# A triangular solve whose products go to PSUM, and expert outputs added to the residual rows by an accumulating scatter

## The reference, cut to what matters

```python
# chunk_gated_delta: 4 heads, both directions
lmat = jnp.where(strict, jnp.einsum('bhnid,bhnjd->bhnij', kb, k) * decay, 0.0)
tinv = lax.linalg.triangular_solve(lmat + eye, eye, left_side=True, lower=True, unit_diagonal=True)
...
# hier_moe: top-1 of 4 groups, top-2 of its 8 experts, blocks of 128 rows for one expert
hdn = jax.nn.silu(xb @ w1[e]) * (xb @ w3[e]);  y = hdn @ w2[e]
y_assign = ybuf[dest] * sw[:, None]                    # the gate
y = jax.ops.segment_sum(y_assign, stok, num_segments=n_tok)
...
x = x + hier_moe(rmsnorm(x, norm2_g), ...);  out = rmsnorm(x, final_norm_g)
```

## Time and profile before

| | |
|---|---|
| median of 3 runs | 3221.87 us (3218.67 to 3228.97) |
| the profiled execution | 3223.99 us, of which its span is 3222.4 us |
| busy in the span | PE 85%, DVE 63%, POOL 35%, ACT 31% |
| bytes moved by DMA | 433.96 MB, 135 GB/s over the span |
| `delta` | about 943 to 1680 us |
| `route` | 1975.7 to 2030 us |
| `experts` | 2030 to 3110.6 us |
| `combine` | 3110.6 to 3222.4 us |

### The profile page before, as it was taken

One profiled execution on the slowest core, in us unless ns is written; L12 is line 12 of the kernel. 1 busy time (PEld: TensorE's weight loads), 2 busy tenths in 40 slices (PEclk: granted clock), 3 DMA queues, 4 the chain that ended last, 5 costly groups with the idle time before them and its releaser, 6 DMA issues. The chain is left out here.

```text
span 3222.4 us, 45930 instructions
## 1 busy us (share of the span) xinstructions
PE 2732.1 (85%) x15152; PEld 2417.5 (75%) x15153; DVE 2039.0 (63%) x2191; ACT 1011.8 (31%) x2067; POOL 1128.5 (35%) x841
## 2 busy tenths in 40 slices
PE   5999999999858888888888995698899999999840
PEld 4998989989747777777776884576787888778730
DVE  5465564655537777777763335879678576877827
ACT  5152351523523333333323221122222323222223
POOL 4110110101035555555522221444354354435424
PEclk9999999999979999999998997799999999999975
DMA  4011120111121111111005441688567565757639
GB/s 151 27 59 41 48 67 29 58 39 48 42 83 53 53 52 52 52 52 52 27 13 173 138 154 52 240 304 317 205 251 272 208 236 215 286 208 293 235 142 359
DMA packets 228387, 433.96 MB, mean 135 GB/s; under 512 B 15065, under 2 KB 104393, under 8 KB 228170
## 3 DMA queue, kind: packets, MB, share of 16 engines
q1 hardware_dynamic: 207336, 349.86, 31.2%
q0 software_dynamic: 13328, 55.06, 4.7%
q10 hardware_dynamic: 7634, 27.79, 2.1%
HBM read 352.75 MB, written 87.25 MB: 137 GB/s over the span
## 5 line engine op out<-in xcount | busy, mean ns | idle before, releaser
L468 PE MATMUL project_proj<-hT_high,project_w_high 128*128 128x412 f32 (+3 forms) x1392 | 496.3, 357 | 28.0 <-issue 10.4
L468 PE MATMUL project_proj<-hT_low,project_w_high 128*128 128x412 f32 (+3 forms) x1392 | 474.9, 341 | 0.0
L468 PE MATMUL project_proj<-hT_high,project_w_low 128*128 128x412 f32 (+3 forms) x1392 | 474.8, 341 | 0.0
L1682 DVE TENSOR_TENSOR experts_w_low<-experts_w_whole,experts_w_high 128x2048 fp32r<-128x2048 f32 x128 | 355.6, 2778 | 4.4
L1776 PE MATMUL experts_h<-experts_w_high,experts_xT_high 128*128 x848 | 340.5, 401 | 18.8 <-DVE experts_w_low L1682 11.8
L1776 PE MATMUL experts_h<-experts_w_low,experts_xT_high 128*128 x848 | 338.9, 400 | 0.0
L1776 PE MATMUL experts_h<-experts_w_high,experts_xT_low 128*128 x848 | 337.5, 398 | 0.0
L1680 DVE CAST experts_w_high<-experts_w_whole 128x2048 fp32r<-128x2048 f32 x128 | 191.6, 1497 | 168.4 <-DMA experts_w_whole<-in_w_dram 168.3
L468 PEld LDWEIGHTS project_proj<-hT_high,project_w_high 128*128 128x128 f32 (+1 forms) x1392 | 261.4, 188 | 45.1 <-issue 31.6
L958 PE MATMUL delta_prep<-delta_Tm,delta_M 128*128 128x128 f32 x1152 | 185.1, 319 | 119.5 <-DVE delta_Tm L1117 116.9
L468 PEld LDWEIGHTS project_proj<-hT_low,project_w_high 128*128 128x128 f32 (+1 forms) x1392 | 261.3, 188 | 14.4 <-issue 9.8
(11 more groups left out here) (282 smaller groups left out, 5814.3 us busy)
## 6 DMA issues: line engine op xcount, KB each, us to landing
experts_w_whole<-in_w_dram SPq DMA_DIRECT2D x128, 1024.0 KB, 10.1
experts_w_whole<-in_w_dram SPq DMA_DIRECT2D x32, 2048.0 KB, 18.6
delta_qkv<-feat SPq DMA_DIRECT2D x36, 768.0 KB, 4.9
y_rows<-experts_yout ACTq DMA_DIRECT2D x53, 512.0 KB
project_w_whole<-in_w_tiles_dram SPq DMA_DIRECT2D x28, 512.0 KB, 4.3
feat<-project_out SPq DMA_DIRECT2D x48, 205.0 KB, 1.9
normalise_x<-in_x_dram SPq DMA_DIRECT2D x18, 512.0 KB, 3.2
delta_row<-gc_rows SPq DMA_DIRECT2D x36, 256.0 KB, 3.3
```

What stands on the lines that cost most here:

```text
L468: r = pe.matmul(dst, w[s][:, kt, 0:m], x[:, kt, lo:hi], start=kt == 0 and i == 0, stop=kt == KD - 1 and i == 2)
L1682: m = dve.tensor_tensor(low, loaded, high.bitcast(F32), ALU.subtract)
```

## The change

The 8x8 substitution writes its products to a PSUM tile of lane 1 that is free at that time (`step8` becomes a view of it), and when it ends, one added copy brings the solved blocks to another part of that tile (`solved8`), from which line 1150 (now 1152) reads. `X8` itself stays in SBUF.

`route` now also brings each slot's gate to the slot, in two parts (the products of line 1585 on DVE, two more columns sets in the PSUM tile), gives empty slots row numbers of 128 spare rows behind the tokens, and does one of the two token-number products on ACT instead of POOL. `output` stores 128 rows more of x2 and of xn for these spare rows.

`experts` scales the output by the slot's gate in the same ACT copies, and instead of ACT's store to `y_rows`, POOL issues an indirect DMA that adds the 128 rows of `yout` to the rows of x2 in DRAM (line 1748). Scatters follow one another by `y_free`. The DMAs that filled unused rows are gone. `combine` becomes `finish`: load x2, norm, store, with 6 buffers instead of 3 and no gathers or sums.

```diff
-        step8, X8 = b.sb("step8", [P, 2 * HEADS, 8]), b.sb("X8", [P, 2 * HEADS, 8])
+        X8 = b.sb("X8", [P, 2 * HEADS, 8])
...
+        step8, solved8 = (L[1]["A"][0][:, n, 0:16 * HEADS].rearrange("p (m r) -> p m r", r=8) for n in range(2))
...
-                dve.wait_ge(base, a * 14 + 14)
+                dve.wait_ge(base, a * 15 + 14)
+                dve.tensor_copy(solved8[:, :, :], X8[:, :, :]).then_inc(base, 1)
+                dve.wait_ge(base, a * 15 + 15)
...
-                    part = bcast(X8[:, d * HEADS:(d + 1) * HEADS, local_view(d)], P // 8, 2)
+                    part = bcast(solved8[:, d * HEADS:(d + 1) * HEADS, local_view(d)], P // 8, 2)
...
+            sp.dma_start(x2_rows[T:T + P, :], x2[1][:, :]).then_inc(x2_st[1], 16)
+            sp.dma_start(xn_rows[T:T + P, :], xn[1][:, :]).then_inc(xn_st[1], 16)
...
-                for i in range(2):
-                    pool.tensor_tensor(marks[c][:, :, i, :], hot_block[c][:, :, :], bcast(tok[:, i, :], MAXB + 2, 2), ALU.mult).then_inc(hot_blocks_set, 1)
+                pool.tensor_tensor(marks[c][:, :, 1, :], hot_block[c][:, :, :], bcast(tok[:, 1, :], MAXB + 2, 2), ALU.mult).then_inc(token_marks, 1)
...
+            for c in range(2):
+                act.wait_ge(hot_set, 2 * c + 1)
+                act.activation(marks[c][:, :, 0, :], hot_block[c][:, :, :], ACT.Copy, scale=tok[:, 0, 0:1]).then_inc(row_marks, 1)
...
+                dve.wait_ge(hot_set, 2 * c + 1)
+                for i, part in ((2, gate_high[:, c].bitcast(F32)), (3, gate_low[:, c])):
+                    dve.tensor_tensor(marks[c][:, :, i, :], hot_block[c][:, :, :], bcast(part, MAXB + 2, 2), ALU.mult).then_inc(gate_marks, 1)
...
-            dve.tensor_copy(idx[:, :], marked[:, :])
...
+            link(dve.tensor_scalar(vacant[:, :], idp[:, 1, :], 0.0, spare[:, 0:1], ALU.is_equal, ALU.mult))
+            dve.scalar_tensor_tensor(out=idx[:, 0:MAXB + 2], in0=marked[:, :], scalar=-float(P), in1=vacant[:, :], op0=ALU.add, op1=ALU.add)
+            link(dve.tensor_copy(slot_gate[:, 0:MAXB + 2], idp[:, 2, :]))
+            dve.tensor_tensor(slot_gate[:, 0:MAXB + 2], idp[:, 3, :], slot_gate[:, 0:MAXB + 2], ALU.add)
...
+            def scatter(blk):
+
+                pool.wait_ge(y_free, blk * 16 + 16)
+                pool.tensor_copy(y_ix, idx[:, bass.ds(blk, 1)]).then_inc(e["y_ix_set"], 1)
+                pool.wait_ge(e["y_ix_set"], blk + 1)
+                pool.wait_ge(e["y_set"], blk + 1)
+                pool.sem_inc(e["scatters_begun"], 1)
+                pool.indirect_dma_start(out=x2_rows[:, :], out_offset=bass.IndirectOffsetOnAxis(ap=y_ix, axis=0),
+                                        in_=yo[:, :], in_offset=None, compute_op=ALU.add).then_inc(y_free, 16)
...
-            def empty_rows(j):
-
-
-                with pool.If(j * -2 + (2 * PAIRS - 1) >= n):
-                    dst = y_rows[bass.ds(j * (-2 * P) + (2 * PAIRS - 1) * P, 2 * P), :]
-                    pool.dma_start(dst, xn_rows[0:2 * P, :]).then_inc(emptied, 16)
-                    pool.wait_ge(emptied, j * 16 + 16)
-
-                pool.sem_inc(e["pairs_through"], 1)
+                if not (isinstance(blk, int) and blk == 0):
+                    scatter(blk - 1)
...
+            pool.dma_start(yo[0:1, :], dram["final_norm_g"].rearrange("(a n) -> a n", a=1)).then_inc(y_free, 16)
...
+            through_blocks(pool, n, step)
+            last = n // 2 * 2
+            gated_low(last)
+            scatter(last)
+            pool.wait_ge(y_free, last * 16 + 32)
...
-            def output(blk):
-
+            def output(q, blk, gated):
+
+                act.activation(y_gate[q], slot_gate[:, bass.ds(blk, 1)], ACT.Copy).then_inc(e["y_gate_set"], 1)
+                act.wait_ge(e["y_gate_set"], blk + 1)
+                act.wait_ge(e["gated_set"], gated)
                 act.wait_ge(y_free, blk * 16 + 16)
                 for c in range(2):
 
                     act.wait_ge(e["done" if c else "y_ready"], blk + (1 + c))
-                    m = act.activation(yo[:, c * 512:(c + 1) * 512], Y[c][:, :], ACT.Copy)
+                    m = act.activation(yo[:, c * 512:(c + 1) * 512], Y[c][:, :], ACT.Copy, scale=y_gate[q])
                 m.then_inc(e["y_set"], 1)
-                act.wait_ge(e["y_set"], blk + 1)
-                act.dma_start(y_rows[bass.ds(blk * P, P), :], yo[:, :]).then_inc(y_free, 16)
...
+            for t in range(NT):
                 sp.wait_ge(e["out_set"], t + 1)
-                sp.dma_start(y[bass.ds(t * P, P), :], out[p][:, :]).then_inc(stored[p], 16)
-
-            def step(p, j, t):
-
-                sp.wait_ge(e["out_set"], t - (U - 1))
-                sp.dma_start(x[p][:, :], x2_rows[bass.ds(t * P, P), :]).then_inc(x_ld[p], 16)
-                store(p, t - U)
-
-            for p in range(U):
-                sp.dma_start(x[p][:, :], x2_rows[p * P:(p + 1) * P, :]).then_inc(x_ld[p], 16)
-            sp.dma_start(gf[:, :], dram["final_norm_g"].partition_broadcast(P)).then_inc(const, 16)
-            through_tiles(sp, 1, NT // U, step)
-            for p in range(U):
-                store(p, NT - U + p)
+                sp.dma_start(y[t * P:(t + 1) * P, :], out[t % U][:, :]).then_inc(stored[t % U], 16)
+                if t + U < NT:
+                    load(t % U, t + U)
...
+        @block.scalar
+        def _(act):
+            for t in range(NT):
+                p = t % U
+                act.wait_ge(x_ld[p], t // U * 16 + 16)
+                act.activation(junk[:, :], x[p][:, :], ACT.Square, accum_out=ss[p][:, :]).then_inc(e["squared"], 1)
+                act.wait_ge(e["squared"], t + 1)
+                if t >= U:
+                    act.wait_ge(e["inverted"], t - U + 1)
+                act.activation(rt[p][:, :], ss[p][:, :], ACT.Sqrt, bias=k["eps"][:, :], scale=1.0 / D).then_inc(e["rooted"], 1)
```

More of the change, by code:

```diff
@@ L57 @@
 MAXB += 1 - MAXB % 2
-SLOTS = MAXB * P
 LEVELS = 7
@@ L1415, in _, with route @@
                     split(p, j * 2 + p)
-def route(nc, k, lg, gate, slot, table, idx):
+def route(nc, k, lg, slot_gate, table, idx):
     with ExitStack() as ctx:
@@ L1445, in route @@
         hot_block = [b.sb(f"hot_block{c}", [P, NT, MAXB + 2]) for c in range(2)]
-        marks = [b.sb(f"marks{c}", [P, NT, 2, MAXB + 2], F32R) for c in range(2)]
+        marks = [b.sb(f"marks{c}", [P, NT, 4, MAXB + 2], F32R) for c in range(2)]
         H = NT // 2
@@ L1601, in experts @@
         ix, xg = pair("ix", [P, 1], I32), b.sb("xg", [P, D])
+        y_ix, y_gate = idx[:, MAXB + 2:MAXB + 3], [slot_gate[:, MAXB + 2 + p:MAXB + 3 + p] for p in range(2)]
         xh = pair("xT_high", [P, KD, P], F32R)
@@ L1633, in through_blocks @@
                     step(0, j * 2 + 2, j + 1)
-                if and_then is not None:
-                    and_then(j)
         @block.sync
@@ L1879, in _, with finish @@
             turned_gate(n // 2 * 2)
-            act.wait_ge(e["gated_set"], n // 2 * 2 + 1)
-            output(n // 2 * 2)
-            act.wait_ge(y_free, n // 2 * 32 + 32)
-            act.sem_inc(e["all_stored"], 1)
-def combine(nc, k, dram, gate, slot, x2_rows, y_rows, y):
+            output(0, n // 2 * 2, n // 2 * 2 + 1)
+def finish(nc, k, dram, x2_rows, y):
     with ExitStack() as ctx:
-        b = Bufs(nc, ctx, "combine_")
-        U = 3
-        ring = lambda name, shape, dt=F32: [b.sb(f"{name}{p}", shape, dt) for p in range(U)]
+        b = Bufs(nc, ctx, "finish_")
+        U = 6
+        ring = lambda name, shape: [b.sb(f"{name}{p}", shape) for p in range(U)]
@@ L1893, in combine @@
         gf, junk = b.sb("final_gain", [P, D]), b.sb("junk_f", [P, D])
-        ix, x, out = ring("cix", [P, 2], I32), ring("cx", [P, D]), ring("out", [P, D])
-        r = [ring(f"crow{c}", [P, D]) for c in range(2)]
-        ss, rt, ri = ring("css", [P, 1]), ring("crt", [P, 1]), ring("cri", [P, 1])
-        names = "ix_set gathers_begun sum1 sum2 squared rooted inverted out_set".split()
-        e = {n: b.sem("fin_" + n) for n in names}
+        x, out = ring("x", [P, D]), ring("out", [P, D])
+        ss, rt, ri = ring("ss", [P, 1]), ring("rt", [P, 1]), ring("ri", [P, 1])
@@ L1899, in combine @@
+        e = {n: b.sem("fin_" + n) for n in "squared rooted inverted out_set".split()}
         const = b.sem("fin_const")
         x_ld = [b.sem(f"fin_x{p}") for p in range(U)]
-        r_ld = [b.sem(f"fin_rows{p}") for p in range(U)]
         stored = [b.sem(f"fin_stored{p}") for p in range(U)]
         block = ctx.enter_context(nc.Block())
-        def through_tiles(eng, first, last, step):
-            with eng.Fori(first, last) as j:
-                for p in range(U):
-                    step(p, j, j * U + p)
@@ L1925, in _, with load @@
-            sp.dma_start(gf[:, :], dram["final_norm_g"].partition_broadcast(P)).then_inc(const, 16)
-            through_tiles(sp, 1, NT // U, step)
-            for p in range(U):
-                store(p, NT - U + p)
+            def load(p, t):
```

(37 more changed lines are left out.)

77 lines of the change are left out of this document (27 added, 50 removed).

## The result

The changed kernel takes 3029.8 us (median of 4 runs, 3024.62 to 3034.35) against 3220.27 (3217.71 to 3228.97, 4 runs, same chip): a ratio of 0.940, 95% interval 0.938 to 0.943. The forecast was 3050, in a range of 3015 to 3110. The profiled execution after has a span of 3022.9 us, before 3222.4, so 199.5 us are to be found in the two traces, some 9 more than in the medians (the traced execution after is the fastest of the four).

The account below looks back on a forecast made before the run. In `delta` DVE's substitution, slowed by two SBUF operands beside POOL, was taken to set the step's end while PE waits for `Tm`. 3224.0 - 135 - 48 + 6 + 3 = 3050 us, range 3015 to 3110.

Parts of the forecast that it names:

- `delta`, -135: `delta`: one operand in PSUM shortens subtractions and R, ends PE's wait and low clock, 7.6 us a step, -135 us.
- The lower bounds: `delta`: no clock gain, -108 us; PSUM writes 0.1 us longer each, -121; by the skill page, total 3068 us.
- Rivals 2 and 3: `delta`: 2, rest of step or low clock holds it, 3077 us, chance 0.14; 3, subtractions stay 959 ns, 3185 us, 0.04.
- The last phase, -53: `combine` becomes `finish`: gathers go, own transfers stay, 59 us instead of 111.8, -53 us.
- The last scatter, +5: Before the last phase: the last block's scatter must land first, 1.0 issue and some 6 landing, +5 us.
- `route` and the ends, +6: `route` +3 us for added products, two more stores at the end of `output` +2, later first gather +1.
- `experts`, +3: `experts`: the scatter's loop stays hidden, extra DMA load costs +3 us; -10 to +40 without the loop.
- rival 4: `experts`: the scatters' extra traffic makes weights land late, +40 us, 3090 us in all; chance 0.09.
- Rival 1, the loop: `experts`: the accumulating scatter's loop becomes the bound, up to 3273 us; chance 0.04 ending slower, 0.03 at a smaller price.
- the sum of 14.4: `experts`: loop from scatter to scatter, landing 10.2 us plus 4.2 us for the rest, under a block's 18 us.
- The sign that the w3 copy waits for PE and not for the scatter: `experts`: ACT's w3 copy should wait for PE as before, the block staying at 18.0 us where PE is full.
- a landing of 16.2 us: `experts`: the scatter landing time from which the loop was said to decide; the whole gain gone at 19.5 us.

Follow-up runs that it names:

- pool_halves: Kernel before, substitution left in SBUF, POOL's operations M, keT and qdT beside it each cut in two: 3126.4 us, ratio 0.972.
- gain_first: Changed kernel, last phase's gain loaded ahead of the x tiles, 9 buffers instead of 6: 3025.7 us; side by side 3028.8 against 3030.4 us.
- no_add: Changed kernel with the scatter writing the rows instead of adding to them: 3027.6 us, ratio 0.941.
- two_scatters: Changed kernel with a second accumulating scatter, to 128 further spare rows, behind each scatter, ACT waiting for both: 3051.2 us, ratio 0.949.

## Why the prediction was right, and where it was off

**`delta`, -135: measured -144.0.** Right in mechanism and in its parts. The step went from 40.96 us (944.83 to 1641.17 in 17 steps) to 32.96 (941.57 to 1501.84): 8.0 instead of 7.6. Idle: I had left 0.2 us for lane 1, and none is left (6.16). Clock: 1.74 instead of 1.65. The first step, for which I had 6.3, gave 6.6 (40.6 to 33.9 us), and the 17 others 8.1 each. The lower bounds named with it did not come: the writes to PSUM cost 6 ns each (198 after 192), not the 100 I had allowed. The Trainium skill, Perfetto Trace Analysis, section Optimizing Scalar/DVE Operations, by which I had weighed 65 ns an operation against the term, gives PSUM the larger overhead; these traces do not show it: besides the 198 after 192, the subtraction of `route` wholly in SBUF took 193 ns, a product of the same size with an operand in PSUM 192. What I gave as the reason, both operands in SBUF beside POOL, is shown by `pool_halves`; that the price is the rest of POOL's running operation I had not seen, though the rows beside the earlier trace rows held it. The forecast does not hang on it: with one operand in PSUM neither a fixed price nor a wait is left.

**Rivals 2 and 3** are excluded by the same rows: subtractions at 185 ns, no wait for `Tm`, clock 1.00.

**The last phase, -53: measured -57.0.** 54.7 us instead of 59; my 6 us for start, pause and end were too many, though the pause is there: 4 us of it went in `gain_first`.

**The last scatter, +5: measured +9.9**, the term that was most off in proportion. I counted 1.0 of issue and some 6 of landing behind it; the landing came 6.1 us after the issue's beginning, so this part was even less. What I had at nothing without a reason is the DRAIN that closes POOL's phase, 5.75 us, up to 2968.0. `no_add` shows that it is not due to the addition: there it takes 9.0 us. In `no_add`, `two_scatters` and the changed kernel it ends 11.7 to 12.5 us after the last block's first scatter begins, whenever the landing comes. What POOL does in it no run here shows.

**`route` and the ends, +6: measured +1.2** for `route`; the two added stores show in nothing (`route` begins 0.9 us after the last logits in both traces), so the 2 us counted for them were wrong.

**`experts`, +3: measured -4.0**, inside its bounds. The extra traffic is there, DMA share 0.73 against 0.66, and costs no time, so rival 4 did not come. The -4.0 is no gain either: three traces with the old tail have 1075.2 to 1078.7 us in this stretch, seven with single scatters 1074.3 to 1080.6. The stretch before `delta` and that of `output` are together 5.7 us shorter, which I lay to no cause either: the runs of one kernel differ by more (3024.6 to 3034.4). The traces fell some 25 us further than the sum (199.5 against 174): `delta` 9, `route` with the stores 5, the last phase 4, `experts` 7 and the stretches beside them 6, less 5 for the last scatter; nearly 10 of that is spread.

**Rival 1, the loop.** That the sum of 14.4 came near is in part luck: two errors cancel. The landing, counted from the issue's beginning as for the gathers, is 8.3 us in the median (11.5 at the longest) where I took 10.2. The reason for the 10.2, that adding moves the bytes twice, was not what makes it long: a scatter that only writes lands in 7.1. The rest of the loop is 6.4 us in the block of `two_scatters` shown, with a POOL product of up to 3.3 us beside DVE where I took 1.3, against my 4.2. 8.3 and 6.4 are 14.7 under a block of 18.0: hidden by 3.3 us instead of 3.6, and with the longest landing, 17.9, just so. The sign that the w3 copy waits for PE and not for the scatter failed in 11 of 53 blocks; `no_add`, without those waits, is not faster. Where the price begins I had too late, at a landing of 16.2, because I set the loop against the mean block of 20.4: `two_scatters`, whose second scatter lands some 12 us after the first begins, already pays 21 to 28 us, about half a microsecond a block.

## What to carry to other kernels

When a small operation costs the same whatever its size, look at what the neighbouring engine runs in that moment and compare the ends: here each 0.2 us subtraction ended with POOL's operation; moving one operand to PSUM took that wait away, and halving POOL's pieces cut it by more than half. Count a wait of PE twice, once as idle and once for the clock after it, where the rows show that it falls. And a loop through a transfer is read from a kernel in which it binds: where it is hidden, its links contain waits for others. Look, too, from where a landing is counted, lest the issue stand in the sum twice.
